# One core of Trainium2, a hybrid decoder layer: mixer inputs laid out by strips and copies during the first product, pooling as moving sums, attention from gate tile 1

## The reference, cut to what matters

```python
(z_nsa_q, z_nsa_kv, z_nsa_g, z_s5, z_pool, z_rq, z_rk, z_rv, z_rg, z_merge) = ...
o_nsa = nsa_mixer(...)   # compressed keys, all blocks selected, window: softmax over 256 keys
o_s5 = s5_mixer(...)     # h_t = A_bar h_(t-1) + B_bar u_t; y = gelu(Re(C h) + D u); GLU
# pooling: for w in (2, 4, 8, 16), a quarter of the columns each
pooled.append((cg[:, 1:] - lower) / count)     # mean of the last w rows, fewer at the start
y = jnp.einsum('bsgc,gcd->bsgd', (pooled - u32), w_pool)
o_ret = retention_mixer(...)  # rotated q and k, decayed scores, norm, silu(gate)
merged = merged + merge_gates[:, :, j] * (o @ w_branch[i, j])
```

## Time and profile before

| what | us |
|---|---|
| median of 3 runs (1586.77 to 1587.53) | 1586.87 |
| the profiled execution | 1587.12 |
| its span | 1585.1 |
| PE busy in the span | 1573.3 (99%) |
| DVE busy | 1055.2 (67%) |
| ACT busy | 921.5 (58%) |
| GpSimd (POOL) busy | 28.1 (2%) |
| mean granted clock of PE, of full speed (2.4 GHz) | 0.998 |

### The profile page before, as it was taken

One profiled execution on the slowest core, in us unless ns is written; L12 is line 12 of the kernel. 1 busy time (PEld: TensorE's weight loads), 2 busy tenths in 40 slices (PEclk: granted clock), 3 DMA queues, 4 the chain that ended last, 5 costly groups with the idle time before them and its releaser, 6 DMA issues.

```text
span 1585.1 us, 19949 instructions
## 1 busy us (share of the span) xinstructions
PE 1573.3 (99%) x7354; PEld 1294.9 (82%) x7354; DVE 1055.2 (67%) x1301; ACT 921.5 (58%) x1367; POOL 28.1 (2%) x53
## 2 busy tenths in 40 slices
PE   9999999999999999999999999999999999999997
PEld 7888888878888888888888888888888888888886
DVE  6547858777999977886656644665555545656665
ACT  7444546665445446657787634773367544777755
POOL 0000022110000000000000000000000000000000
PEclk9999999999999999999999999999999999999999
DMA  9686555555676677867656556656666556655653
GB/s 330 202 294 205 178 185 185 172 166 183 209 216 207 192 225 272 270 234 259 202 179 205 197 193 196 189 188 202 195 185 199 196 189 187 197 198 193 220 197 122
DMA packets 163555, 325.33 MB, mean 205 GB/s; under 512 B 10768, under 2 KB 16016, under 8 KB 162576
## 3 DMA queue, kind: packets, MB, share of 16 engines
q1 hardware_dynamic: 163328, 324.22, 63.7%
q10 hardware_dynamic: 144, 0.01, 0.0%
HBM read 313.70 MB, written 10.49 MB: 205 GB/s over the span
## 4 chain that ended last, share of the span: by engine, by line
PE 99%; ACT 0%; DMA 0%; DVE 0%; issue 0%; ACTq 0%
PE ps L402 32%; PE ps L404 31%; PE ps L403 31%; PE ps L662 0%; PE ps L668 0%; PE ps L665 0%; PE ps L774 0%; PE ps L826 0%; PE ps L873 0%; PE ps L809 0%; PE ps L968 0%; PE ps L966 0%; PE ps L967 0%; DMA sb<-in_xt 0%; PE ps L884 0%; PE ps L730 0%
## 5 line engine op out<-in xcount | busy, mean ns | idle before, releaser
L385 DVE TENSOR_TENSOR sb<-sb,sb 128x1024 fp32r<-128x1024 f32 x552 | 673.1, 1224 | 432.8 <-ACT sb L378 422.9
L378 ACT ACTIVATE sb<-sb 128x1024 fp32r<-128x1024 f32 x552 | 582.0, 1057 | 504.3 <-PE ps L404 470.4
L402 PE MATMUL ps<-sb,sb 128*128 128x512 f32 (+1 forms) x2192 | 854.3, 390 | 0.4 <-issue 0.4
L403 PE MATMUL ps<-sb,sb 128*128 128x512 f32 (+1 forms) x2192 | 850.2, 388 | 0.0
L404 PE MATMUL ps<-sb,sb 128*128 128x512 f32 (+1 forms) x2192 | 850.1, 388 | 0.0
L402 PEld LDWEIGHTS ps<-sb,sb 128*128 128x128 f32 x2192 | 411.4, 188 | 88.9 <-issue 3.1
L404 PEld LDWEIGHTS ps<-sb,sb 128*128 128x128 f32 x2192 | 411.4, 188 | 85.1
L403 PEld LDWEIGHTS ps<-sb,sb 128*128 128x128 f32 x2192 | 411.6, 188 | 82.9
L457 ACT ACTIVATE ps<-ps 32x256 f32<-32x256 f32 x464 | 162.8, 351 | 42.5 <-DVE ps L446 36.6
L446 DVE STREAM_TRANSPOSE ps<-sb 128x512 f32<-128x512 f32 x58 | 38.1, 702 | 0.2
L1767 DVE TENSOR_TENSOR sb<-sb 128x1024 f32<-128x1024 f32 x16 | 19.6, 1225 | 25.1 <-ACT sb L1183 25.1
(11 more groups left out here) (241 smaller groups left out, 534.0 us busy)
## 6 DMA issues: line engine op xcount, KB each, us to landing
sb<-in_w_in SPq DMA_DIRECT2D x128, 512.0 KB, 3.8
sb<-in_w_up SPq DMA_DIRECT2D x128, 512.0 KB, 3.8
sb<-in_w_down SPq DMA_DIRECT2D x128, 512.0 KB, 4.3
sb<-in_w_mix SPq DMA_DIRECT2D x56, 512.0 KB, 3.9
sb<-in_w_branch SPq DMA_DIRECT2D x32, 512.0 KB, 5.4
sb<-in_w_out SPq DMA_DIRECT2D x32, 512.0 KB, 4.4
sb<-in_w_pg SPq DMA_DIRECT2D x32, 512.0 KB, 4.3
gate_mem<-sb SPq DMA_DIRECT2D x16, 512.0 KB, 6.2
```

The lines of the kernel that those rows point to most:

```text
L378: act.activation(whi[:, j % RING, :], raw[:, j % RING, :], ACT.Copy).then_inc(hi_done, 1)
L385: eng.tensor_tensor(wlo[:, j % RING, :], raw[:, j % RING, :], whi[:, j % RING, :].bitcast(F32), ALU.subtract).then_inc(lo_done, 1)
L402: pe.matmul(o, xh, w_h, start=first and k == 0, stop=False)
L403: pe.matmul(o, xh, w_l, start=False, stop=False)
```

## The change

What it does: the transposes on PE of kv, q, k, the compressed probabilities and the retention's result go. DVE turns these in strips into one of two buffers `lanes` (`turn`), and GpSimd (`move`, seven jobs of 16 copies) or, for q, ACT (`move_q`, 32 copies, 4 per tile) places the blocks. Most of it is done at fixed (i, j) of the first product. Pooling: DVE makes sums over 2, 4, 8 and 16 rows by doubling (`window_sums`), corrects the first rows and subtracts (`pool_inputs`); the product with `w_pool` and its split move into unit 6, compression to unit 3, selection to unit 4. The rotations move to unit 7. Attention starts at gate tile 1 (A_CS), heads 5 tiles apart, the retention two tiles and the scan four tiles sooner. `s5p` is loaded in unit 1, `w_cmp` and `cmp_sel` after unit 1, with SP's wait for the squares. In the branch stage ACT's moves and both splits of the merged result come one or two tiles later.

```diff
-TP_RET, TP_GLU, TP_M = 0, 1, 2
+TP_GLU, TP_M = 0, 1
...
-A_BAND, A_POOL, A_SEL, A_QTR, A_KTR, A_CS, A_PCT = 2, 4, 6, 7, 8, 9, 13
-A_HEAD = [14 + 4 * i for i in range(NH)]
...
+Z_KV, Z_Q, Z_CMP, Z_PART, Z_U5, Z_SEL, Z_XG, Z_PL = (2, 1), (3, 1), (3, 5), (3, 7), (4, 2), (4, 4), (4, 6), (5, 1)
+Z_SUMS, Z_MIX, Z_SPLIT = (6, 0), (6, 4), (6, 6)
+Z_ROT = [(7, 0), (7, 2), (7, 4), (7, 6)]
+Z_RQ, Z_RK = (7, 5), (8, 4)
+J_KV, J_Q, J_U5, J_PL, J_RQ, J_RK, J_PC, J_RY = range(8)
+A_CS = 1
+A_HEAD = [A_CS + 4 + 5 * i for i in range(NH)]
 A_RTR = A_HEAD[-1] + 5
 A_RS = [A_RTR + 2 + i for i in range(RH)]
-A_U5 = A_RS[-1] + 1
-A_RQUAD = A_U5 + 2
-A_S5 = [A_RQUAD + 2 + 8 * n for n in range(8)]
+A_RY = A_RS[-1] + 2
+A_S5 = [A_RY + 1 + 8 * n for n in range(8)]
...
+        def turn(v, n, src, blocks=4):
+            if n == J_U5:
+                v.wait_ge(sg["moved"], 1)
+            elif n == J_PL:
+                v.wait_ge(sg["q_moved"], 1)
+            elif n > J_PL:
+                v.wait_ge(sg["moved"], n - 2)
             for tt in range(TT):
+                dst = lane_strips(n, blocks)[:, :, tt, :, :].rearrange("p r k m -> p k r m")
+                ins = v.transpose(dst, src(tt).rearrange("p (k r m) -> p k r m", k=blocks, r=4))
             ins.then_inc(sg["lane_done"], 1)
+        def move(gp, n, dst, blocks=4):
             gp.wait_ge(sg["lane_done"], n + 1)
             for i in range(16):
                 q, r = i // 4, i % 4
+                ins = gp.tensor_copy(dst[32 * r:32 * r + 32, :, :, 32 * q:32 * q + 32],
+                                     lane_strips(n, blocks)[32 * q:32 * q + 32, r])
             ins.then_inc(sg["moved"], 1)
...
+                    if (i, j) == (1, 2):
+                        sp.dma_start(s5p[:, :, :], a["s5p"]).then_inc(s5p_in, 16)
                 if i == 1:
-                    sp.dma_start(s5p[:, :, :], a["s5p"]).then_inc(const_in, 16)
                     sp.dma_start(ident[:, :], a["ident"]).then_inc(const_in, 16)
...
-                if i == 3:
                     sp.wait_ge(x_lo, TPU)
                     sp.wait_ge(ssq_done, TT)
                     sp.dma_start(w_cmp[:, :, :], a["w_cmp"]).then_inc(cmp_in, 16)
                     sp.dma_start(cmp_sel[:, :, :], a["cmp_sel"]).then_inc(cmp_in, 16)
...
+            def pool_mix():
+                pe.wait_ge(pool_in, 48)
+                pe.wait_ge(sg["pool_summed"], 1)
+                for g in range(4):
+                    mm = pe.matmul(aux[0][:, g * S:(g + 1) * S], w_pool[:, g, :], x_pad[:, g, PAD:PAD + S],
+                                   start=True, stop=True)
+                mm.then_inc(sg["pool_mixed"], 1)
...
             pe.wait_ge(s5_b_in, 16)
-            pe.wait_ge(tp_lo, TP_RET + 1)
+            pe.wait_ge(sg["ret_done"], 1)
             s5_inputs(0)
...
+                    t = (i - Z_Q[0]) * TPU + j - Z_Q[1] - 1
+                    if 0 <= t < 8:
+                        for n in range(4 * t, 4 * t + 4):
+                            move_q(n)
...
-                        turned(j, TP_M + n - 1, (n - 1) % 2)
-                    if j == 4 and n:
+                        turned(j - 1, TP_M + n - 1, (n - 1) % 2)
+                    if j == 5 and n:
                         merged_hi(n - 1)
...
+            move(gp, J_KV, by_block(kv_t))
+            move(gp, J_U5, z_cols(S50))
+            gp.wait_ge(sg["cmp_sum"], 1)
+            move(gp, J_PL, by_block(x_pad[:, :, PAD:PAD + S]))
+            move(gp, J_RQ, z_cols(RQ0))
+            move(gp, J_RK, z_cols(RK0))
+            move(gp, J_PC, pc_t.rearrange("p g t q -> p t g q"), NG)
+            move(gp, J_RY, ry.rearrange("p t (k m) -> p t k m", k=4))
...
+            def window_sums(k):
+                w, g = 2 ** k, k
+                src, dst = (x_pad if k == 0 else sums[(k - 1) % 2]), sums[k % 2]
+                link(v.tensor_tensor(dst[:, g:4, PAD:PAD + S], src[:, g:4, PAD:PAD + S], src[:, g:4, PAD - w:PAD + S - w],
+                                     ALU.add))
+            def pool_inputs():
+                for k in range(2):
+                    link(v.tensor_tensor(sums[k][:, k:4:2, PAD:2 * PAD], sums[k][:, k:4:2, PAD:2 * PAD],
+                                         pool_fix[:, k:4:2, :], ALU.mult))
+                for g, w in enumerate(WINDOWS):
+                    x = x_pad[:, g, PAD:PAD + S]
+                    ins = v.scalar_tensor_tensor(out=x, in0=sums[g % 2][:, g, PAD:PAD + S], scalar=1.0 / w, in1=x,
+                                                 op0=ALU.mult, op1=ALU.subtract)
+                ins.then_inc(sg["pool_summed"], 1)
...
+                    if i == Z_SUMS[0] and 0 <= j - Z_SUMS[1] < 3:
...
+                        if n == 0:
...
+                            window_sums(0)
+                        if n == 1:
+                            window_sums(1)
+                            window_sums(2)
+                        if n == 2:
+                            window_sums(3)
+                            v.wait_ge(pool_in, 48)
+                            pool_inputs()
...
             i.then_inc(sg["ret_done"], 1)
-            until(A_RQUAD)
-            quad_lo(v, TP_RET, 1, o_lo[:, 12:16, :], o_hi[:, 12:16, :])
-            v.wait_ge(tp_lo, TP_RET + 1)
+            v.wait_ge(sg["ret_done"], 1)
+            turn(v, J_RY, lambda tt: ry[:, tt, :])
+            def ret_low():
+                v.wait_ge(sg["ret_hi"], 1)
+                v.tensor_tensor(by_block(o_lo[:, 12:16, :]), ry[:, :, :].rearrange("p t (k m) -> p t k m", k=4),
+                                by_block(o_hi[:, 12:16, :].bitcast(F32)), ALU.subtract).then_inc(sg["ret_lo"], 1)
...
                 until(A_S5[n] + 5)
+                if n == 0:
+                    ret_low()
...
-                    if n and j == 4:
+                    if n and j == 6:
                         merged_lo(n - 1)
```

More of the change, by code:

```diff
@@ L683, in _ @@
             until = interleaved(gate_tile)
[L684 to L704, removed]
@@ L705, in _ @@
-            mm.then_inc(sg["pool_mixed"], 1)
-            pe.wait_ge(cmp_in, 32)
-            pe.wait_ge(sg["cmp_copied"], 1)
-            for b0 in range(0, 16, 4):
-                for i in range(4):
-                    mm = pe.matmul(aux[1][32 * i:32 * i + 32, C:C + 2 * P], kv_ct[:, :, b0 + i:S:16],
-                                   w_cmp[:, b0 + i:32:16, :], start=b0 == 0, stop=b0 == 12)
-            mm.then_inc(sg["cmp_sum"], 1)
-            until(A_SEL)
-            pe.wait_ge(sg["cmp_sb"], 1)
@@ L717, in _ @@
-            for g in range(NG):
-                for i in range(2):
-                    pe.matmul(aux[1][:, g * DH:(g + 1) * DH], cmp_sel[:, 2 * g + i, :], cmp_part[:, i, P:P + DH],
-                              start=i == 0, stop=i == 1)
-            for g in range(NG):
-                for i in range(2):
-                    mm = pe.matmul(aux[1][:, P + g * CP:P + (g + 1) * CP], cmp_part[:, i, 0:P],
-                                   cmp_sel[:, 2 * g + i, 0:CP], start=i == 0, stop=i == 1)
@@ L786, in _ @@
             scores(0)
[L787 to L793 removed]
+            pe.wait_ge(const_in, 48)
             for hd in range(NH):
@@ new lines, in pool_low, with rotate @@
+            def pool_low():
+                v.wait_ge(sg["pool_hi"], 4)
+                for g in range(4):
+                    i = v.scalar_tensor_tensor(out=o_lo[:, 8 + g, :], in0=aux[0][:, g * S:(g + 1) * S],
+                                               scalar=pool_s[:, g:g + 1], in1=o_hi[:, 8 + g, :].bitcast(F32),
+                                               op0=ALU.mult, op1=ALU.subtract)
+                i.then_inc(sg["pool_lo"], 1)
+            def rotate(i):
+                c0, tt = (RQ0, RK0)[i // 2], i % 2
+                if i == 0:
+                    v.wait_ge(rot_in, 16)
+                else:
+                    v.wait_ge(sg["rot_done"], i)
+                v.wait_ge(grp_free, 2 * ((c0 + BW - 1) // C + 1))
+                x = z[:, tt, c0:c0 + BW]
+                heads = x.rearrange("p (h d) -> p h d", h=RH)
+                sw = x.rearrange("p (h i two) -> p h i two", h=RH, two=2)[:, :, :, ::-1]
+                cs = rot[:, 0, tt:tt + 1, :].to_broadcast([P, RH, P])
+                sn = rot[:, 1, tt:tt + 1, :].to_broadcast([P, RH, P])
+                link(v.tensor_tensor(rtmp[:, :].rearrange("p (h i two) -> p h i two", h=RH, two=2), sw,
+                                     sn.rearrange("p h (i two) -> p h i two", two=2), ALU.mult))
+                link(v.tensor_tensor(heads, heads, cs, ALU.mult))
+                v.tensor_tensor(x, x, rtmp[:, :], ALU.add).then_inc(sg["rot_done"], 1)
@@ L1749, in _ @@
                         strips(v, (NCH - 1) % 2, lambda tt: merged[:, tt * C:(tt + 1) * C])
-                    if n == 0 and j == 4:
+                    if n == 0 and j == 5:
                         merged_lo(NCH - 1)
```

420 lines of the change are left out of this document (192 added, 228 removed).

## The result

| | before | after |
|---|---|---|
| median of the runs, us | 1587.22 (1586.77 to 1587.53, 8 runs) | 1591.54 (1590.15 to 1592.66, 8 runs) |
| profiled execution, us | 1587.12 | 1590.15 |
| its span, us | 1585.1 | 1588.4 |

The ratio is 1.0026, with a 95% interval of 1.0018 to 1.0035: slower by about 0.26%, a small change, but its interval leaves out 1. It was predicted as 1586.9, in a range up to 1591.0.

What follows compares the result with a forecast made beforehand. PE was taken as the bound, side work being free until it uses up the lead of the split tiles. Savings and new waits summed to +0.1 us, so 1586.9 us by the median, range 1582.5 to 1591.0.

Steps and rivals of the forecast that it cites:

- step 7: Scans' start: GpSimd's copies of the retention's result lengthen DVE's operations with two SBUF inputs, +1.5 us (0.7 to 2.1).
- step 4: Pooling as moving sums in unit 6: DVE done at 148.0, PE asks at 147.59; +0.45 us (0 to 1).
- step 3: w_cmp and its selector loaded ahead of unit 2, not unit 4: the tile behind them is late, +0.55 us (0 to 5.2).
- Step 1: PE loses banding products, transposes and the retention's quad: 6.77 us less, with +0.10 for one further stop.
- Step 2: Branch products: ACT's moves and the merged result's splits a tile or two later, -0.90 us (0 to -0.99).
- Step 5: Attention from gate tile 1, heads every 5 tiles: +0.75 us at head 2 (0 to 1.5), +0.20 at head 0.
- Its second term: Head 0 comes one tile earlier behind the compressed softmax, GpSimd's copies taking most of its lead: +0.20 us (0 to 1).
- Step 6: Start of the scans: PE needs them sooner and DVE is late, PE with it, +4.2 us (3 to 5).
- the sign that the prediction set itself: PE's waits between gate tiles 54 and 62, on DVE's splits, sum to 5 to 6 us; under 2 or over 8 refutes.
- Rival C: Early loads of w_cmp find no lead, PE waits 5.2 us in place of 0.55: 1591.6; chance 0.07.
- A: Rival: the scans' start has room, no loss there from DVE's lateness or GpSimd's copies: 1581.2; chance 0.15.
- rival B: Each of 16 retention copies stands its whole 0.39 us in DVE's way, 6.2 in place of 1.5: 1591.6; chance 0.13.

Runs made afterwards that it cites:

- the last version: Changed kernel with all helpful edits, scans four tiles later, VectorE splitting further ahead, retention's low part in the scan's second step: 1579.24 us, ratio 0.9951.
- the run with one copy: Changed kernel with only one of the 16 GpSimd copies of the retention's result, so that result isn't laid out: 1588.70 us.

## Why the prediction was wrong

The sum came to +0.1 us and the span grew by 3.3; the median grew by 4.3. The places and the engine that ends PE's waits (VectorE) came out as forecast. What failed is what the sum left out or put too small: the wait of ScalarE for GpSimd's last copy in step 7, put at nothing (1.5 us), a split and a copy out of PSUM in step 4 (+1.9 in place of +0.45), and the loads of step 3 (+1.5 in place of +0.55).

| step | predicted | by the tiles of the profile |
|---|---|---|
| 1, PE's work | -6.67 | -6.8 |
| 2, branch stage | -0.90 | -0.8 |
| 3, loads of w_cmp | +0.55 | +1.5 |
| 4, pooling | +0.45 | +1.9 |
| 5, heads | +0.95 | +0.8 |
| 6 and 7, scans' start | +5.7 | +7.1 |
| start of the kernel, not in the sum | 0 | -0.3 |

The rows come to 3.4, beside the 3.3 of the span.

**Step 1** held: the last version, which has no wait of PE but those of the start, is 7.74 us shorter in its span than the kernel before, of which 0.8 are the branch stage and 0.1 the start. The start itself differs from run to run: the last tile ahead of unit 2 began between 46.52 and 47.71 us in the 15 profiled runs, so a tenth or two in these rows means nothing. **Step 2** held; the idle piece went, and a slow start of 0.2 us stayed. **Step 5** held, with the chain as told: sigmoids, table, exponentials, then the scaling, done 8.87 us behind the start of tile 15 (8.85 worked out). Its second term, 0.20 for head 0, did not show: no wait of PE stands there.

**Step 7** failed by what it left out. It priced the copies' disturbance of VectorE (1.5 predicted, 1.1 found) and said nothing of who waits for their end. ScalarE's high part does, with every later split behind it in the queue, and that cost another 1.5 us through VectorE's idle time. GpSimd's job was also longer than the 9.81 us of the earlier trace rows, 13.12. Its copies stretch beside VectorE's work, as their durations (ns, least/median/most) show:

```profile
L485 POOL COPY sb<-sb x112: 285/398/1807, 59.8 to 388.3; 32x256 f32<-32x256 f32 x96, 32x128 f32<-32x128 f32 x16
```

**Step 6** held as a size, as far as a difference shows it: 7.1 less 1.1 and 1.5 leaves 4.5, where 4.2 were predicted. The 3.1 us that two tiles brought once ScalarE's wait was gone fit the same account. By the sign that the prediction set itself, waits of 5 to 6 us there, the 5.0 us of listed waits looked nearly right; only the lengths of the tiles show the 7.1.

**Step 4** took its start from the earlier trace rows and counted three splits. The stretch held a fourth, and the copy of a unit's result out of PSUM stood in it as well (VectorE's order of time in the kernel after):

```profile
143.35 1.23 DVE L396 TENSOR_TENSOR sb<-sb,sb 128x1024 fp32r<-128x1024 f32 x1
144.49 0.75 DVE L1352 TENSOR_SCALAR sb<-ps,sb 128x512 f32<-128x512 f32 x1
145.15 1.22 DVE L396 TENSOR_TENSOR sb<-sb,sb 128x1024 fp32r<-128x1024 f32 x1
...
153.02 1.43 DVE L1393 SCALAR_TENSOR_TENSOR sb<-sb,sb 128x256 f32<-128x256 f32 x4
```

Those two are 1.8 us, and the sums were otherwise a little quicker than priced: 1.73 of idle time instead of 0.45. Moving a piece of work into a stretch means listing all that already stands between its first and its last instruction.

**Step 3** had the landing nearly right (ScalarE split the tile at 48.27, where 48.1 was worked out), but PE came 0.3 earlier than in the earlier trace rows, and one number was given for what differs from run to run: unit 2's second tile started between 52.96 and 56.99 in the nine profiled runs with the loads early. Rival C named this place; its reason, that no lead is there, holds in part, its 5.2 us in none of the nine: the most was 4.6, of which 1.7 was the clock.

**The clock** was in no step, and it makes the rest of the median. A stretch of 3.41 us at half clock lowers the mean granted clock of this span by 0.0011, enough to be seen in a run's rounded mean: of the 15 profiled runs the four with such a fall have 0.997, the eleven without have 0.998 or 0.999. Of the kernel after's eight runs three have 0.998 (1590.15, 1590.56, 1590.85) and five 0.997 (1591.23 to 1592.66), and the medians of the two groups are 1.8 us apart, where a fall costs some 1.6. So five of eight runs probably held a fall that the profiled one didn't. It is also the likely reason why the removal of the loads' or the pool's wait brought 1 us more by the medians than by the tiles: among the runs at 0.998 or more alone it brought 1.6 and 2.3 (1590.56 to 1588.96 and 1588.28), close to the 1.5 and 1.95 of the tiles. No profile of a run of the kernel after with a fall was at hand, so that much is inferred.

**The rivals.** A fell: VectorE was the last to be ready, as forecast. B and C both gave the right time, 1591.6, for the wrong reason; that is luck. The copies did not cost VectorE their whole 0.39 us each, and the run with one copy brought 2.5 us in all, not over 4. The Trainium skill, SBUF — State Buffer, section Who interferes with whom, calls the port pair that VectorE and GpSimd share an exclusive lock; it names operations of VectorE with two SBUF inputs as contending with a GpSimd one that reads SBUF, and says of VectorE's two-port modes that whoever issues first holds the pair for the whole instruction. This trace agrees that the two contend (copies of GpSimd took up to 1.81 us in place of 0.39) and that a PSUM input spares VectorE. It does not bear out the price that rival B drew from it, since VectorE lost 0.07 to 0.23 us an operation.

## What to carry to other kernels

For every moved step list who waits for its last instruction and what is queued behind that waiter: here copies on GpSimd, the idlest engine, held up ScalarE, and through it VectorE and PE. Where two engines are late at the same place, an edit for one of them may show little (here 0.25 and 1.5 us, and 4.6 together); try them together before dropping either. Where PE waits 2 us in one place, a loss of clock may come on top in some runs: read the tiles of the profile beside the medians.

## What was not expected of the hardware

TensorE's granted clock fell to 0.50 (1.2 GHz) for one stretch of 3.41 us in four of the 15 profiled runs (the last 6 to 10 us apart, behind PE's last product, where it falls in every one), each time behind a wait of PE (2.74, 2.68, 1.86 and 1.77 us), and each cost 1.6 to 1.7 us on top of the wait. Waits of 1.43 and 1.78 us in the kernel after were followed by none, so waits of the same length can go either way; what decides it is not shown. Even without a fall the first product behind a wait is slow: 0.47 or 0.50 us in place of 0.39.

VectorE's small operations were also slower beside GpSimd's copies, with one input too: a TENSOR_SCALAR of 128x16 took 408 ns on the mean beside the second job, 175 before it (groups of the kernel after, from 99 to 107 us and from 108 to 117.4):

```profile
L1326 DVE TENSOR_SCALAR sb<-sb 128x16 f32<-128x16 f32 x3 | 0.5, 175 | 0.1
```

```profile
L1326 DVE TENSOR_SCALAR sb<-sb 128x16 f32<-128x16 f32 x2 | 0.8, 408 | 0.1
```
